# Differential attention of an encoder trunk: transposes and value products taken one unit later, a second pair of buffers for the exponentials

## The reference, cut to what matters

```python
def diff_mixer(q, k, v, q_head_g, k_head_g, lam, out_g, lambda_init, cos, sin):
    q = apply_partial_rope(rms_norm(q.reshape(b, t, 2 * DIFF_HEADS, DIFF_QK), q_head_g), cos, sin)
    k = apply_partial_rope(rms_norm(k.reshape(b, t, 2 * DIFF_HEADS, DIFF_QK), k_head_g), cos, sin)
    ...
    def attend(qb):
        p = softmax_probs(qb, k, scale).reshape(b, DIFF_HEADS, 2, qb.shape[1], t)
        amap = p[:, :, 0] - lam_full * p[:, :, 1]
        return jnp.einsum('bhqk,bkhd->bqhd', amap.astype(v.dtype), v)

    o = sweep_query_blocks(attend, q)
    o = rms_norm(o, out_g) * (1.0 - lambda_init)
    return o.reshape(b, t, DIFF_HEADS * DIFF_V)
```

## Time and profile before

| | |
|---|---|
| time, median of 3 runs | 2227.95 us (2227.86 to 2228.83) |
| the profiled execution | 2227.46 us |
| its span in the trace | 2225.7 us |
| TensorE busy over the span | 2045.0 us (92%) |
| VectorE, ScalarE, GpSimd busy | 49%, 37%, 45% |
| granted TensorE clock, mean | 0.975 of full speed |
| chain of work that ended last | TensorE 75%, VectorE 12%, ScalarE 7% |

### The profile page before, as it was taken

One profiled execution on the slowest core, in us unless ns is written; L12 is line 12 of the kernel. 1 busy time (PEld: TensorE's weight loads), 2 busy tenths in 40 slices (PEclk: granted clock), 3 DMA queues, 4 the chain that ended last, 5 costly groups with the idle time before them and its releaser, 6 DMA issues.

```text
span 2225.7 us, 32546 instructions
## 1 busy us (share of the span) xinstructions
PE 2045.0 (92%) x13234; PEld 1767.1 (79%) x13234; DVE 1084.8 (49%) x1737; ACT 820.9 (37%) x1344; POOL 996.1 (45%) x593
## 2 busy tenths in 40 slices
PE   7999998888778999999989999988887799999999
PEld 7988986567667999999989889875565577888887
DVE  7542475565665644441037433665655655444400
ACT  3322353676553222222223222534665533222221
POOL 4365443774213344444434554436843134444443
PEclk9999999999999999999999999999999899999999
DMA  4211111000001222323322112120000013333333
GB/s 163 67 58 58 58 58 57 10 1 29 20 20 48 86 96 86 95 86 95 105 74 83 63 48 67 48 76 10 1 19 29 20 58 94 95 95 95 95 104 114
DMA packets 40036, 143.80 MB, mean 65 GB/s; under 512 B 4432, under 2 KB 4560, under 8 KB 39760
## 3 DMA queue, kind: packets, MB, share of 16 engines
q1 hardware_dynamic: 39888, 141.72, 20.0%
HBM read 139.60 MB, written 2.10 MB: 64 GB/s over the span
## 4 chain that ended last, share of the span: by engine, by line
PE 75%; DVE 12%; ACT 7%; issue 4%; POOL 1%; DMA 1%; SPq 0%; DVEq 0%; ACTq 0%; POOLq 0%
PE pb L853 35%; PE pb L888 7%; PE pb L889 7%; PE pb L890 7%; PE pb L926 4%; PE pb L928 3%; PE pb L927 3%; ACT ebuf L1481 2%; PE pb L1300 2%; DVE rowmax L1950 1%; PE pb L1308 1%; ACT rstd L1449 1%; PE pb L1012 1%; PE pb L1240 1%; ACT ebuf L1492 1%
## 5 line engine op out<-in xcount | busy, mean ns | idle before, releaser
L636 POOL TENSOR_TENSOR parts<-raw,parts 128x1024 fp32r<-128x1024 f32 x248 | 604.4, 2438 | 800.2 <-ACT parts L1537 800.1
L1537 ACT ACTIVATE parts<-raw 128x1024 fp32r<-128x1024 f32 x248 | 262.6, 1059 | 835.0 <-PE pb L853 413.5
L853 PE MATMUL pb<-proj_r,parts 128*128 128x264 f32 x3104 | 429.1, 286 | 0.5 <-POOL parts L636 0.5
L853 PEld LDWEIGHTS pb<-proj_r,parts 128*128 128x128 f32 x3104 | 401.0, 189 | 0.8 <-issue 0.7
L853 PE MATMUL pb<-mix,parts 128*128 128x264 f32 x2208 | 338.9, 295 | 28.4 <-POOL parts L636 15.8
L853 PEld LDWEIGHTS pb<-mix,parts 128*128 128x128 f32 x2208 | 301.8, 195 | 35.1 <-issue 17.1
L926 PE MATMUL pb<-mix,parts 128*128 128x264 f32 x800 | 241.5, 302 | 1.3 <-DVE proj L1880 1.3
L928 PE MATMUL pb<-mix,parts 128*128 128x264 f32 x800 | 228.5, 286 | 0.0
L927 PE MATMUL pb<-mix,parts 128*128 128x264 f32 x800 | 228.1, 285 | 0.0
L888 PE MATMUL pb<-proj_r,parts 128*128 128x512 f32 x528 | 207.5, 393 | 0.8 <-DVE mbuf L1871 0.8
L890 PE MATMUL pb<-proj_r,parts 128*128 128x512 f32 x528 | 207.7, 393 | 0.0
(11 more groups left out here) (286 smaller groups left out, 3308.1 us busy)
## 6 DMA issues: line engine op xcount, KB each, us to landing
raw<-w_stream SPq DMA_DIRECT2D x250, 512.0 KB, 3.5
w_head<-w_heads SPq DMA_DIRECT2D x8, 512.0 KB, 4.9
h<-x_t SPq DMA_DIRECT2D x8, 264.0 KB, 7.0
out_t<-h SPq DMA_DIRECT2D x8, 256.0 KB, 4.5
con<-consts SPq DMA_DIRECT2D x1, 1652.5 KB, 10.5
par<-params SPq DMA_DIRECT2D x1, 340.0 KB, 4.5
con<-consts SPq DMA_DIRECT2D x1, 128.0 KB, 7.0
```

Source lines behind the costliest of these rows:

```text
L636: nc.gpsimd.tensor_tensor(parts[:, n % PARTS, 1, :], w, parts[:, n % PARTS, 0, :].bitcast(FP32), ALU.subtract).then_inc(split.sem, 1)
L853: last = nc.tensor.matmul(pb[rows_, 2 * p + a, 0:HALF], lhs_t, rhs[:, a * HALF:(a + 1) * HALF], start=start, stop=stop)
L1537: nc.scalar.activation(parts[:, n % PARTS, 0, :], raw[:, r % RAW, :], ACT.Copy).then_inc(lead_ready.sem, 1)
```

## The change

Four things move in the loop over units, in both layers.

- **Transposes a unit later.** In pass `u` of the loop, TensorE now transposes unit `u - 1` right behind the scores of unit `u + 1`; ScalarE and VectorE read out unit `u - 1` at the end of their pass. The loop has one pass more.
- **Exponentials of odd units in `kh`.** Latent attention's key buffer is free by then; `maps_of(u)` gives `kh` for odd and `ebuf` for even units, and `softmax` waits for the difference of two units before instead of one.
- **Both maxima ahead of the difference.** VectorE's pass is now: inverse sums of `u`, maxima of `u + 1`, difference of `u`, read-out of `u - 1`. ScalarE scales the second map of `u` at the start of its pass.
- **Value products a unit later.** `attend` stands at the second tile of the next head instead of the first, and ScalarE may only overwrite `PT_LEAD` of a new head once it has ended (a new wait on `o_ps`). The norm's steps and the pieces of the output projection move back with it, `normed_out` from the third tile to the fourth. The last `attend` now stands between two halves of group `G_OUT2 - 1`.

```diff
         def dense_part(layer, u):
-            hp, i = u // n_q(layer), u % n_q(layer)
-            ...
-            return (None, (0, 2), (2, 4), (4, 6), (6, 8))[i]
+            if u < n_q(layer):
+                return 0, value_part(u) if layer < DEPTH - 1 else ((0, 2), (2, 4), (4, 6), (6, 8))[u]
+            hp, at = (u - 2) // n_q(layer), (u - 2) % n_q(layer)
+            return (hp, ((0, 2), (2, 5), (5, 8))[at]) if at < 3 and 1 <= hp < DIFF_H else (hp, None)
+
+        def maps_of(u):
+
+            return kh if u % 2 else ebuf
...
-                for u in range(diff_units(l)):
+                for u in range(diff_units(l) + 1):
                     hp, i = u // n_q(l), u % n_q(l)
                     if 0 < u < diff_units(l) - 1:
                         score_pair(u + 1)
-                    if i == 0 and hp:
+                    if u:
+                        turn(n_att_m(l) + u - 1)
+                    if i == 1 and hp:
                         pe.wait_ge(evac.sem, evac.at(l, G_OUT1 + 3 + hp))
                         attend(MLA_H + hp - 1)
-                    turn(n_att_m(l) + u)
-                    if i == 1 and hp:
+                    if i == 2 and hp:
...
-                pe.wait_ge(evac.sem, evac.at(l, G_OUT2 - 1))
+                beside(l, G_OUT2 - 1, 0, mixed_parts, ((0, KD // 2),))
                 attend(N_MAP - 1)
-                beside(l, G_OUT2 - 1, 0, mixed_parts, ((0, KD),))
+                beside(l, G_OUT2 - 1, 0, mixed_parts, ((KD // 2, KD),))
...
-                    act.wait_ge(map_ready.sem, map_ready.at(l, n_att_m(l) + u))
+                    act.wait_ge(map_ready.sem, map_ready.at(l, n_att_m(l) + max(u - 1, 0)))
...
+                if m > MLA_H and i == 0:
+                    act.wait_ge(o_ps.sem, o_ps.at(l, m))
...
+                    if 0 < u < diff_units(l):
+                        inverse_sums(l, u)
                     if u + 1 < diff_units(l):
                         row_max(l, n_att_m(l) + 2 * u + 2)
                         row_max(l, n_att_m(l) + 2 * u + 3)
...
+                    if 0 < u < diff_units(l):
+                        difference(l, u)
+                    if u:
+                        turned_rests(l, n_att_m(l) + u - 1)
...
-                    if i == 2 and hp:
+                    if i == 3 and hp:
                         dve.wait_ge(rs_ready.sem, rs_ready.at(l, RS_OD + hp))
                         normed_out(l, tile_of(proj, DV + hp - 1), gain_d[:, :])
```

More of the change, by code:

```diff
@@ L1491, in scaled_second @@
                 act.wait_ge(r_ready.sem, r_ready.at(l, n_att_m(l) + u + 1))
-                nc.scalar.activation(ebuf[:, 1, :], ebuf[:, 1, :], ACT.Copy, scale=rsum[:, 1:2]).then_inc(second_scaled.sem, 1)
+                second = maps_of(u)[:, 1, :]
+                nc.scalar.activation(second, second, ACT.Copy, scale=rsum[:, 1:2]).then_inc(second_scaled.sem, 1)
             def turned_leads(l, u):
@@ L1785, in _ @@
                 rsqrt(l, SQ_A + 4, 3, 512, rstd2)
-                for u in range(diff_units(l)):
+                for u in range(diff_units(l) + 1):
                     hp, i = u // n_q(l), u % n_q(l)
-                    if i or hp == 0:
-                        turned_leads(l, n_att_m(l) + u)
+                    if 0 < u < diff_units(l):
+                        scaled_second(l, u)
                     if u + 1 < diff_units(l):
                         softmax(l, n_att_m(l) + 2 * u + 2)
-                        if i == 1 and hp:
+                        if i == 2 and hp:
                             log_dif(l, hp - 1)
                         softmax(l, n_att_m(l) + 2 * u + 3)
-                        scaled_second(l, u + 1)
+                    if u:
+                        turned_leads(l, n_att_m(l) + u - 1)
+                    if i == 2 and hp:
+                        root_exp(rstd2)
                     if i == 1 and hp:
-                        root_exp(rstd2)
-                    if i == 0 and hp:
                         out_dif(l, hp - 1)
-                        turned_leads(l, n_att_m(l) + u)
-                    if i == 0:
+                    if i == 0 and hp < DIFF_H:
                         lead(l, S_OUT1 + 4 + hp)
@@ L1971, in difference @@
                 dve.wait_ge(t_ps.sem, t_ps.at(l, n_att_m(l) + max(u - 1, 0)))
-                nc.vector.scalar_tensor_tensor(out=mbuf[:, u % 2, 0:T], in0=ebuf[:, 0, :], scalar=rsum[:, 0:1], in1=ebuf[:, 1, :],
+                nc.vector.scalar_tensor_tensor(out=mbuf[:, u % 2, 0:T], in0=maps_of(u)[:, 0, :], scalar=rsum[:, 0:1], in1=maps_of(u)[:, 1, :],
                                                op0=ALU.mult, op1=ALU.add).then_inc(map_ready.sem, 1)
@@ L2384, in _ @@
                         row_max(l, n_att_m(l) + 2 * u + 3)
-                    if i or hp == 0:
-                        turned_rests(l, n_att_m(l) + u)
-                    if i == n_q(l) - 1:
-                        residual(l, G_OUT1 + 3 + hp, 3 + hp)
-                    if u + 1 < diff_units(l):
-                        inverse_sums(l, u + 1)
-                        difference(l, u + 1)
-                    if i == 0 and hp:
-                        turned_rests(l, n_att_m(l) + u)
+                    if 0 < u < diff_units(l):
+                        difference(l, u)
+                    if u:
+                        turned_rests(l, n_att_m(l) + u - 1)
+                    of, part = dense_part(l, u)
+                    if part and part[1] == KD:
+                        residual(l, G_OUT1 + 3 + of, 3 + of)
                     if u == 0:
```

14 lines of the change are left out of this document (6 added, 8 removed).

## The result

| | before | after |
|---|---|---|
| time, median | 2228.39 us (4 runs, 2227.86 to 2235.58) | 2206.59 us (4 runs, 2201.82 to 2208.49) |
| the profiled execution, its span | 2227.46, 2225.7 us | 2201.82, 2200.0 us |
| granted TensorE clock, mean | 0.975 | 0.981 |
| layer 0's loop, first to last maximum | 105.89 us | 91.20 us |
| layer 1's loop | 92.04 us | 70.80 us |

The ratio of the times is 0.9897, with a 95% interval of 0.9872 to 0.9921: 1.0% faster, 22 us by the medians and 25.6 us between the two profiled executions. The forecast was 2210 us, with 2197 to 2223 as its range. At its own places the change gives, between the two profiled executions: 14.7 us less in layer 0's loop, 21.2 less in layer 1's, 1.5 and 6.8 more at the ends. Together 27.6.

What follows compares the result with a forecast made beforehand. In the loops the serial chain from engine to engine was taken as the bound, no engine being full. Loop gains 17.9 and 19.1, ends +0.4 and -5.3, made 32.1; minus 14 for the clock, 2228 - 18 = 2210 us, range 2197 to 2223.

Steps and rivals of the forecast that it cites:

- Passes: Loops over units: an ordinary pass falls from 4.70 to 4.08 us; a layer-0 head takes 24.88.
- Layer 1: Layer 1's loop: 73.0 us instead of 92.0, a gain of 19.1.
- the value product's transposes wait for that edge (6.43): Layer 1's pass with the value product: its transposes wait for the 16-token edge, making the pass 6.43 us.
- Ends: After each loop GpSimd's weight split decides: layer 0 gains 0.4 us, layer 1 loses 5.3.
- The clock: TensorE at half rate after gaps: 2.2 us at five places in the loops, 1.5 at both ends, 14 charged.
- The sum: Whole kernel: 17.9 + 19.1 + 0.4 - 5.3 = 32.1 us, less 14 for the clock, gives 18.
- Clock full: Rival: TensorE's clock stays full because gaps get shorter on the mean; 2196 us, chance 0.13.
- all slow time on the path: Rival: all of today's half-rate TensorE time falls on the path, costing 26 us; 2222 us, chance 0.17.
- GpSimd: Rival: VectorE's difference meets GpSimd's `mixed_split` in fifth passes, 0.5 us in each of six heads; 2213 us, chance 0.10.
- Chain keeps its length: Rival: ScalarE's read-out holds VectorE 0.6 us longer, so ordinary passes stay at 4.70; 2227 us, chance 0.08.
- half rate throughout: Rival: TensorE stays at 1.2 GHz through whole heads and is the bound again; 2241 us, chance 0.05.

Runs made afterwards that it cites:

- the kernel with the added work: Changed kernel plus twelve products that nobody reads in layer 0's first-tile passes of the later heads: 2197.74 us, ratio to the kernel before 0.9856.
- the kernel with the weights first: Changed kernel with GpSimd's split of a group's weights ahead of the split of a head's output at the loops' ends: 2198.36 us, ratio to before 0.9861.
- the shortened kernel before: Kernel before without the value product's ten products a head (five in layer 1) that use the maps' rest part: 2234.70 us, ratio 1.0019.
- the kernel with all three: Changed kernel with GpSimd's weights first, four output pieces in layer 0's later heads, unread products in each layer's second head: 2192.55 us, ratio to before 0.9823.
- with the difference first: Changed kernel with VectorE's difference moved ahead of the maxima again: 2248.68 us, ratio to the kernel before 1.0072.

## Why the prediction was right, point by point

- **Passes.** The ordinary pass is 3.98 us, not 4.08: the inverse sums take 0.33 behind a busy VectorE, where I took the 0.42 that they need behind a wait. The 4.70 that I set against it is no pass of the kernel before: the one without extra work (583.86 to 588.34) took 4.48, those of the later heads 5.4 to 6.7. What was won is better read by heads: the five passes of layer 0's third head took 29.73 us before (633.55 to 663.28, with the half-rate stretch of the earlier trace rows in them) and take 24.97 now. In a layer-0 head the passes are 3.78, 5.99, 5.15, 4.67 and 5.38, against 3.79, 6.01, 5.02, 4.76 and 5.30. At full clock the loop of layer 0 was to be 88.0 and was 88.04, in the kernel with the added work.
- **Layer 1.** The loop is 70.80, not 73.0. The failed step is "the value product's transposes wait for that edge (6.43)": the edge ends earlier than I had it, and the transposes start 0.7 us ahead of the maximum (1731.03 and 1731.72). Two such passes were 5.55 and 5.21; the first one, 6.81, holds a half-rate spell.
- **Ends.** GpSimd decides, as said, with 2.13 and 2.91 us of waiting. The last step came at 28.3 and 30.7. By the prediction it was 26.4 and 29.2 and the clock's 1.5 at each, 27.9 and 30.7. Both half groups begin at or fall to half rate (0.50 from 678 to 681, and from 1770.5 to 1773), which costs 1.5 and 1.2 against the kernel with the weights first.
- **The clock**, the term that was mis-sized. I charged 14 us. In the profiled execution it is 3.2 in layer 0's loop (91.20 less 88.04), about 1.4 in layer 1's (the pass of 6.81 against 5.2 to 5.5) and 2.8 at the ends: 7.4. The charge at the ends held. What failed is the assumption that each of the five places in the loops gets a full spell of 2.2. One place was none: at the end of the first head the clock is 1.00 up to 602. Of the other four, three had a spell, of 1.6, 1.5 and about 1.4 us. Where one fell fully behind a gap it cost 2.6, and in the kernel with the weights first all three gaps of layer 0 had such a one, so the price was near and the count was not. The gaps are 3.15 us, where I had 3.7. The Trainium skill, "TensorE: Matmul & The Clock Gate" (What's actually happening), has the throttled state as the default and activity as what releases it; I took from it that each long gap is followed by a slow stretch. The trace agrees only in part, since 3.15 us of standing still are followed by scores of 1.16 us at 628.12, and by 2.13 at 604.10 in the kernel with the weights first.
- **A gain that I had without naming it.** In the kernel before, the third passes of layer 1's heads took 6.40 us in one of the later heads and 10.11 and 10.15 in the two others, where the whole piece ran at half rate:

```profile
1752.40:1762.30 9.90, 8.90 (x26) 6.05 (x26) 3.40 (x9) 4.26 (x9) 0.00 (x0) 0.52 0.00 1
```

  They are 5.17 and 5.14 now. With the second pair of buffers alone all three of these passes took 6.40. So 7.5 of layer 1's 21.2 us are time given back by the clock, not a shorter chain. The sum held them, since it took the loop's measured length off, but the text spoke of the clock as a cost only.
- **The sum.** Without the clock the terms were 17.9, 19.1 and -4.9 (both ends), together 32.1; the profiled execution gives 17.9, 22.6 and -5.5, together 35.0. The clock takes 7.4 of it and not 14, and 2.0 are lost elsewhere: 25.6, where the forecast had 18.1. Of the 7.5 between them, 6.6 are the clock's charge and 3.5 layer 1's loop, less 0.6 at the ends and the 2.0. The medians are 21.8 us apart, and the new one is 3.4 under the forecast of 2210. That the median came so near is in part luck: the profiled execution, from which the terms are measured, is the fastest of the four and 8.2 us under the forecast.

The rivals. *Clock full* (2196) and *all slow time on the path* (2222) are both out, but the first is near: with only layer 0's three gaps filled the kernel is at 2197.74. *GpSimd*: the difference met `mixed_split`'s second half, as worked out,

```profile
621.62 1.31 POOL L668 TENSOR_TENSOR proj_r<-proj,mix 128x528 fp32r<-128x528 f32 x1
621.78 1.71 DVE L1980 SCALAR_TENSOR_TENSOR mbuf<-kh,rsum 128x528 f32<-128x528 f32 x1
622.88 2.82 POOL L638 TENSOR_TENSOR parts<-raw,parts 128x1024 fp32r<-128x1024 f32 x1
```

and took 1.71 instead of 0.77 us (1.63 to 1.71 in four places). But the pass is 5.38 against the 5.30 worked out without it. VectorE's read-out starts with the difference's end, at 623.41; behind ScalarE's (622.59), spaced as in the ordinary pass, it would have started at 623.21. So a meeting costs about 0.2 us a head and not 0.5. The Trainium skill, "SBUF — State Buffer" (Who interferes with whom), has the later instruction wait for the other; the trace agrees for the difference behind L668, and L638, started 0.6 us before the difference's end, took 2.82 instead of 2.34. It hardly does for the first half (L666, L664 before), which reads SBUF too: the difference at 591.39 began 0.28 us behind such an instruction, took 0.90 and ended before it. *Chain keeps its length* and *half rate throughout* are out by the passes and by the clocks of 0.95 and 0.96.

Open: why layer 0's loop begins 1.16 us later than before and 1.1 us are lost between the loops, in code that is the same in both.

## What to carry to other kernels

When a chain of engines and not one engine sets the pace, order, buffers and the delay of the consumer have to move together: here each pair of the three was slower than the old kernel, by 18 to 65 us, and the buffers alone were worth nothing. Ask of each idle stretch of TensorE not only whether it is on the path but what it does to the clock of the work behind it: a useful piece moved into gaps of 3 us gave 6 us, even unread products gave 7 in one layer (and nothing in the other), and ten hidden products taken out made a kernel slower. A price of half-rate time taken from one trace holds for the place but not for how often it is paid; put the count into the range.

## What the runs showed of the hardware that I had not expected

- A gap of the same length at the same place of a head is followed by a half-rate spell in one case and by none in another: scores of 1.16, 1.22 and 1.53 us behind 3.15 us of standing still in the three later heads of one execution, and of 2.13 in others. A gap of 2.5 us can do it as well: it is followed by scores of 1.53 us in layer 1 of the changed kernel (1707.80), and by a sum of squares of 1.81 in the shortened kernel before. In the kernel with all three the clock fell in layer 1 behind gaps of only 1.05 and 0.73 us (1700.06 and 1701.95).
- Taking ten hidden products a head out of the kernel before lowered the mean clock of its two loops, from first to last maximum, from 0.90 and 0.85 to 0.85 and 0.84 and made it 0.2% slower.
- VectorE's difference of two SBUF maps takes 0.77 us alone. Where it began inside a GpSimd instruction with two inputs it ended 0.56 to 0.58 us after that one's end: in nine places of the changed kernel's loops (0.83 to 1.71 us), in five of the kernel before (1.30 and 1.93) and once with the difference first (2.43). Only where it began 0.15 us before that one's end did it take its 0.77 (1706.85). Where it began inside GpSimd's one-input instruction it took 0.77 to 0.90.
